# A two-step S5 recurrence and a reordered opening in a two-layer decoder kernel

## The reference, cut to what matters

```python
mag = exp(lr * dt); abar_r = mag * cos(li * dt); abar_i = mag * sin(li * dt)
bbar_r = fr * br - fi * bi; bbar_i = fr * bi + fi * br     # per group and state
bu_r = einsum('bsgc,gpc->bsgp', ug, bbar_r)                # bu_i alike
x[s] = abar * x[s-1] + bu[s]                               # complex, 256 steps, as an associative scan
y = einsum(xr, c_re) - einsum(xi, c_im) + d_skip * ug
y = gelu(y); y * sigmoid(y @ w_glu + b_glu)
```

## Time and profile before

| | |
|---|---|
| runs | 1571.39, 1573.44, 1573.77 us; median 1573.44 |
| profiled execution | span 1566.3 us from first to last instruction; no separate device time is kept for it, so 7.1 us of the median lie around its span |
| busy | PE 95%, DVE 82%, ACT 66%, POOL 7% |
| mean granted TensorE clock | 0.986 |
| chain that ended last | PE 80%, DVE 5%, ACT 4% |

### The profile page before, as it was taken

How to read it: one execution, slowest core, us unless ns; L and a number is a source line. 1 busy time by engine, 2 the same in 40 slices (tenths; PEclk the granted TensorE clock), 3 DMA queues, 4 the chain that set the end, 5 groups by cost and what they waited for, 6 DMA issues and landing times.

```text
span 1566.3 us, 21687 instructions
## 1 busy us (share of the span) xinstructions
PE 1489.2 (95%) x7201; PEld 1160.6 (74%) x7202; DVE 1288.4 (82%) x1776; ACT 1027.9 (66%) x1325; POOL 113.8 (7%) x112
## 2 busy tenths in 40 slices
PE   3999999999899899999999999999999999999987
PEld 1645468888795478878888888888888888888865
DVE  6896458785586369899999999989989989989987
ACT  3104444443456457887787788787888888888765
POOL 5251000000000000000001001001001001001030
PEclk9899999999899999999999999999999999999998
DMA  9733968874564289999999999999999999999960
GB/s 309 274 108 138 386 253 294 310 257 161 190 215 164 106 315 392 389 339 386 386 348 384 390 346 379 389 356 373 384 358 373 385 365 368 387 365 367 383 232 28
DMA packets 209930, 482.81 MB, mean 308 GB/s; under 512 B 8084, under 2 KB 14534, under 8 KB 209750
## 3 DMA queue, kind: packets, MB, share of 16 engines
q1 hardware_dynamic: 205872, 468.91, 81.3%
q0 software_dynamic: 3360, 12.10, 2.1%
q10 hardware_dynamic: 646, 1.16, 0.3%
HBM read 474.27 MB, written 7.86 MB: 308 GB/s over the span
## 4 chain that ended last, share of the span: by engine, by line
PE 80%; DVE 5%; ACT 4%; issue 2%; DVEq 0%; ACTq 0%
PE ps L864 23%; PE ps L866 23%; PE ps L865 23%; PE ps L870 3%; DVE w_lo L2056 3%; PE ps L1399 2%; PE ps L1156 2%; ACT work L1947 1%; PE ps L889 1%; ACT w_hi L1686 1%; PE ps L1127 0%; PE ps L958 0%; PE ps L1345 0%; ACT uT L1699 0%; PE ps L984 0%
## 5 line engine op out<-in xcount | busy, mean ns | idle before, releaser
L2056 DVE TENSOR_TENSOR w_lo<-ring,w_hi 128x1024 fp32r<-128x1024 f32 (+2 forms) x572 | 676.5, 1214 | 80.6 <-ACT w_hi L1686 61.7
L1686 ACT ACTIVATE w_hi<-ring 128x1024 fp32r<-128x1024 f32 (+2 forms) x572 | 596.0, 1052 | 222.6 <-PE ps L866 220.6
L864 PE MATMUL ps<-w_hi,e_hi 128*128 128x512 f32 x896 | 356.2, 398 | 5.5 <-DVE w_lo L2056 5.5
L866 PE MATMUL ps<-w_hi,e_lo 128*128 128x512 f32 x896 | 349.5, 390 | 0.0
L865 PE MATMUL ps<-w_lo,e_hi 128*128 128x512 f32 x896 | 348.8, 389 | 0.0
L2056 DVE TENSOR_TENSOR w_lo<-ring_more,w_hi 128x1024 fp32r<-128x1024 f32 x192 | 232.1, 1223 | 16.0 <-ACT w_hi L1686 7.0
L1686 ACT ACTIVATE w_hi<-ring_more 128x1024 fp32r<-128x1024 f32 x192 | 202.7, 1060 | 47.6 <-PE ps L866 47.6
L864 PEld LDWEIGHTS ps<-w_hi,e_hi 128*128 128x128 f32 x896 | 168.3, 188 | 42.1 <-DVE w_lo L2056 9.6
L866 PEld LDWEIGHTS ps<-w_hi,e_lo 128*128 128x128 f32 x896 | 168.1, 188 | 36.1
L865 PEld LDWEIGHTS ps<-w_lo,e_hi 128*128 128x128 f32 x896 | 168.5, 188 | 32.7
L864 PE MATMUL ps<-w_hi,eT_hi 128*128 128x512 f32 x448 | 176.7, 395 | 12.6 <-DVE w_lo L2056 12.6
(11 more groups left out here) (308 smaller groups left out, 1579.8 us busy)
## 6 DMA issues: line engine op xcount, KB each, us to landing
ring<-in_moe_w_gate SPq DMA_DIRECT2D x96, 1024.0 KB, 7.2
ring<-in_moe_w_up SPq DMA_DIRECT2D x80, 1024.0 KB, 7.2
ring<-in_moe_w_down SPq DMA_DIRECT2D x64, 1024.0 KB, 7.2
ring<-in_w_ada SPq DMA_DIRECT2D x24, 2048.0 KB, 12.6
ring_more<-in_moe_w_down SPq DMA_DIRECT2D x48, 1024.0 KB, 7.5
ring_more<-in_moe_w_up SPq DMA_DIRECT2D x32, 1024.0 KB, 7.6
ring_more<-in_moe_w_gate SPq DMA_DIRECT2D x16, 1024.0 KB, 7.6
ring<-in_ff_w_gate SPq DMA_DIRECT2D x5, 2048.0 KB, 8.2
```

Of the source, the lines that this page charges most:

```text
L864: mm(o, xh, wh, start=start, stop=False)
L866: return mm(o, xl, wh, start=False, stop=stop)
L1686: fn(w, src, ACT.Copy).then_inc(hi_ready, 1)
L2056: V.tensor_tensor(w_lo[0:n, c, 0:f], src, w_hi[0:n, c, 0:f].bitcast(F32), ALU.subtract).then_inc(lo_ready, 1)
```

## The change

In the S5 stage two steps of the recurrence are taken as one. With u split into even and odd steps, the state at odd steps obeys x[2k+1] = abar^2 x[2k-1] + (abar * bbar) u[2k] + bbar u[2k+1]; the scan has 128 steps (HS), the tables have 128 columns with doubled angle (so the levels are 0 to 6), and the factor is mag^2. The outputs at odd steps come from C x, those at even steps from (C * abar) x of the step before plus a direct product (C * bbar) u. So `drive(jp)` makes 8 products of 128 columns for the two chunks j0 and j0 + 4 of a pair, `turn(jp)` handles both, and `read_out(jp0)` has 36 products of 127 or 128 columns, four times instead of eight. New are: `ab_bar` and `ca` on POOL, `ab_pads` and `s5_direct_out` on ScalarE, `s5_direct` on TensorE, and two more weights (8 transposes) in `s5_transposes`.

The opening is reordered: SP starts with the conditioning items and loads x before the fourth; c, a_re, a_im, log_dt, b_ada and the small table go to ACT's queue; POOL loads the S5 matrices before the router's weights. TensorE gets 68 products of the identity by itself (`keep_busy`) between the conditioning products, `norm_first` comes after `matvec(3)`, and `s5_transposes` after `s_proj(1)`.

```diff
@@ sync
-            small("c", A["c"]); small("a_re", ...); small("a_im", ...)
-            sp.dma_start(bias_rows[0:BROWS, :], ...)
             for e in static_before[:n_first]:
+                if e is static_before[n_first - 2]:
+                    sp.dma_start(h[:, :, :], x_tok).then_inc(x_in, 16)
                 load(e)
@@ gpsimd (C and B are loaded ahead of w_r and b_r)
+            mul(par(MAG2), par(MAG), par(MAG))
...
+            for i, (x, y, op) in enumerate(((0, 1, ALU.subtract), (1, 0, ALU.add))):
+                mul(s5_t, f(AI), b_bar[:, y, :, :])
+                mul(ab_bar[:, i, :, :], f(AR), b_bar[:, x, :, :])
+                step.wait()
+                nc.gpsimd.tensor_tensor(ab_bar[:, i, :, :], ab_bar[:, i, :, :], s5_t, op).then_inc(ab_ready, 1)
+            pool.wait_ge(s5_wT_ready, 5)
...
+            mul(ca_t, fw(AI), mci)          # each of the next is 128 x 512
+            mul(ca[0], fw(AR), cr)
+            add(ca[0], ca[0], ca_t)
+            affine(ca[1], ca[0], -1.0, 0.0)
+            mul(ca_t, fw(AI), cr)
+            mul(ca[2], fw(AR), mci)
+            nc.gpsimd.tensor_tensor(ca[2], ca[2], ca_t, ALU.subtract).then_inc(ca_ready, 1)
+            for jp in range(NJP):           # 8 pairs, two 128 x 512 products each
...
@@ tensor
             def s5_transposes():
                 pe.wait_ge(s5_pads, 8)
-                for i, bank in enumerate((5, 6, 7, 4)):
+                for i, bank in enumerate((5, 6, 7, 4, 5, 6)):
...
+                    if i == 4:
+                        pe.wait_ge(s5_pads, 12)
+                        pe.wait_ge(s5_wT_ready, 2)
+            def keep_busy(n, bank):
+                for _ in range(n):
+                    mm(ps[bank][:, 0:P], ident, ident, start=True, stop=True)
             matvec(0, 4)
+            keep_busy(6, 2)
+            columns_of(0, parts0[:, 0, :], 4, 0)
+            keep_busy(10, 2)
             matvec(1, 5)
-            columns_of(0, parts0[:, 0, :], 4, 0)
-            norm_first()
+            keep_busy(6, 2)
+            columns_of(1, parts0[:, 1, :], 4, 4)
+            keep_busy(10, 2)
             pe.wait_ge(s5_dt, 1)
             matvec(2, 6)
-            columns_of(1, parts0[:, 1, :], 4, 4)
+            keep_busy(6, 2)
+            columns_of(2, parts0[:, 2, :], 4, 8)
+            keep_busy(30, 2)
             matvec(3, 7)
-            columns_of(2, parts0[:, 2, :], 4, 8)
+            norm_first()
             columns_of(3, parts0[:, 3, :], 4, 12).then_inc(mod_summed, 1)
-            pe.wait_ge(part_ready, 4)
-            s5_transposes()
...
+            def s5_direct():
+                pe.wait_ge(s5_wT_ready, 5)
+                for t in range(4):
+                    o = ps[7][:, t * P:(t + 1) * P]
+                    mm(o, b_pad[:, 0, t, :], s5_cT[:, 0, t, :], start=True, stop=False)
+                    w = mm(o, b_pad[:, 1, t, :], s5_cT[:, 2, t, :], start=False, stop=True)
+            def drive(jp):
...
+                for n, j in enumerate(j_pair(jp)):     # j0 = (jp // 4) * 8 + jp % 4, and j0 + 4
+                    t, r = j // 4, slice(32 * (j % 4), 32 * (j % 4) + 32)
+                    u = halves_of(t, r)                # s_inT[r, t, :] as even and odd steps
+                    for i in range(2):
+                        o = bank[:, (2 * n + i) * HS:(2 * n + i + 1) * HS]
+                        mm(o, s5_abT[r, i, t, :], u[:, 0, :], start=True, stop=False, tile_position=(r.start, 0))
+                        w = mm(o, s5_bT[r, i, t, :], u[:, 1, :], start=False, stop=True, tile_position=(r.start, 0))
+            def read_out(jp0):                         # waits: post_ready; ca_ready, k_ready (0); y_pre 2 (4)
+                for n in range(2):
+                    for jp in pairs: mm(o, s5_kT[:, t, r], halves_of(t, slice(0, P))[:, 0, :], ...)
+                    for i in range(4): for jp in pairs: mm(o, s5_caT[:, c, t, r], x[:, 0:HS - 1], ...)
+                    for i in range(4): for jp in pairs: mm(o, s5_cT[:, c, t, r], x, ...)
             s_proj(0)
             s_proj(1)
+            s5_transposes()
             s_proj(2)
+            s5_direct()
             drive(0)
-            drive(1)
             s_proj(3)
-            drive(2)
-            for jp in range(8):
-                for s in range(6 * jp, 6 * jp + 6):
+            drive(1)
+            for i in range(8):
+                for s in range(6 * i, 6 * i + 6):
                     qkv(s)
-                for j in (2 * jp + 3, 2 * jp + 4): ... drive(j)
-                if jp:
-                    read_out(2 * jp - 2)
+                if i + 2 < NJP:
+                    drive(i + 2)
+                if i in (2, 4, 6):
+                    read_out(i - 2)
             qk_transposes(0)
             qk_transposes(1)
             scores_pair(0, qT, kT, 0, True)
-            read_out(NCH - 2)
+            read_out(NJP - 2)
@@ scalar: order of the opening
-            norm_stats(0); part_out(0), (1); pads(); part_out(2), (3); norm_first_out(); s5_weights(); s_in copies
+            part_out(0), (1); c_pads(); roots(); part_out(2); norm_stats(0); b_pads(); part_out(3)
+            norm_first_out(); ab_pads(); s_in_out(0); s5_weights(range(7)); s5_direct_out(); s_in_out(1)
@@ vector
-            for n in range(5, NLEV): level(n)          # columns and norm_first_out inside level(7)
+            level(5); columns(0, 0, 1, 4); norm_first_out(); level(6)
-                    w = V.tensor_tensor_scan(z[:, i, :], ... MAG ... [P, S], ...)        # 2 of 256 a chunk
+                        w = V.tensor_tensor_scan(z[:, n, i, :], ... MAG2 ... [P, HS], ...)   # 4 of 128 a pair
+            y_before_gelu(0), (1) after turn(6); (2), (3) after the first two mask_max
```

More of the change, by code:

```diff
@@ L257, in trunk @@
         pT = WU.take(2, KW)
-        phase = phase_buf[:, :, :].rearrange("p a (b c) -> p a b c", b=NCH)
+        phase = phase_buf[:, 0, :].rearrange("p (a b c) -> p a b c", a=2, b=NCH)
+        WS = Region(phase_buf[:, 1, :], SLOT)
+        s5_abT = WS.take(2, 4, P)
+        s5_caT = WS.take(3, 4, P)
+        ab_pad = WS.take(2, 4, P)
+        ab_bar = WS.take(2, NCH, C_S5)
         WI = Region(ada[:, 2 * 4 * S:2 * 4 * S + 2048], 2048)
@@ L296, in trunk @@
         late_in = sem("late_in")
-        fill = [sem(f"slot{i}_filled") for i in range(NS1)]
+        fill = [sem(f"slot{i}_filled") for i in range(NS0)]
         half_fill = [[sem(f"slot{i}_half{j}_filled") for j in range(2)] for i in range(NS1)]
@@ L1047, in drive, with halves_of @@
+            def halves_of(t, r):
+                return s_inT[r, t, :].rearrange("p (k l) -> p l k", l=2)
+            def drive(jp):
+                if jp == 0:
+                    pe.wait_ge(s5_wT_ready, 7)
                     pe.wait_ge(vs_ready, 1)
[L1048 removed]
+                if jp == 4:
                     pe.wait_ge(vs_ready, 2)
[L1050 to L1055 removed]
@@ L1400, in o_out_part @@
                 w.then_inc(mix_out_done, 1)
-            def keep_busy(n, bank):
-                for _ in range(n):
-                    mm(ps[bank][:, 0:P], ident, ident, start=True, stop=True)
             def router(t):
@@ L2219, in _ @@
                 norm_scale(0, t, t + 1)
-            for n in range(5, NLEV):
-                level(n)
+            level(5)
+            columns(0, 0, 1, 4)
+            dve.wait_ge(mod_ready, 1)
+            norm_first_out()
+            level(6)
             def rope0(i):
@@ L2253, in turn @@
+                if jp >= 2:
+                    dve.wait_ge(post_ready, jp - 1)
+                z = zbuf[:, jp % 2]
+                for n, j in enumerate(j_pair(jp)):
+                    for i in range(2):
+                        w = V.tensor_tensor_scan(z[:, n, i, :], s5_p[:, MAG2, j:j + 1].broadcast_to([P, HS]), s5_v2[:, n, i, :],
+                                                 0.0, ALU.mult, ALU.add)
+                        if (n, i) != (1, 1):
+                            step(w)
                 w.then_inc(z_ready, 1)
-                dve.wait_ge(z_ready, j + 1)
+                dve.wait_ge(z_ready, jp + 1)
@@ L2259, in y_before_gelu @@
                                        ALU.mult, ALU.add).then_inc(y_pre, 1)
-            for j in range(NCH):
-                turn(j)
-                if j % 4 == 2 and j >= 6:
-                    y_before_gelu(j // 4 - 1)
-                if j in (7, 8, 12, 13):
-                    rope0({7: 0, 8: 1, 12: 2, 13: 3}[j])
+            for jp in range(NJP):
+                turn(jp)
+                if jp in (3, 4):
+                    rope0(jp - 3)
+                if jp == 6:
+                    y_before_gelu(0)
+                    y_before_gelu(1)
+                if jp in (6, 7):
+                    rope0(jp - 4)
```

228 lines of the change are left out of this document (127 added, 101 removed).

## The result

| | before | after |
|---|---|---|
| first comparison, median (runs) | 1573.49 us (1571.39 to 1573.77, 4) | 1585.74 us (1584.10 to 1587.30, 4) |
| ratio, 95% interval | | 1.0078 [1.0064, 1.0092] |
| repeated later | 1572.63 us (11 runs) | 1584.42 us (6 runs), 1.0073 [1.0055, 1.0091] |
| span of the profiled execution | 1566.3 us | 1585.5 us |
| mean granted TensorE clock | 0.986 | 0.984 |

A forecast was written before the change was run, and what follows sets the result against it. TensorE was taken to set the S5 stage, with VectorE costing it 1.8 us. Stage plus 9.8 and opening plus 1.6 gave plus 11.4 on 1573.4: 1584.8, say 1584.5 us; range 1573 to 1594.

The forecast's parts named there:

- VectorE costs the stage 1.8 us and its relief is worth no more: S5 stage: TensorE waits for VectorE only twice, 0.67 and 1.08 us; about 30 us less VectorE work saves only 1.8.
- Drives plus 4.8: S5 drives on TensorE: eight pairs at 1.93 us in one row group, 15.4 against 10.6 before, plus 4.8 us.
- Read-outs plus 1.6: S5 read-outs on TensorE: four at 4.1 us, 16.4, against eight at 1.85, 14.8; plus 1.6 us.
- Transposes plus 2.95, direct product plus 1.8: S5 stage on TensorE: 24 transposes now between two projections add 2.95 us, the direct product's 16 records 1.8.
- The tail plus 0.45: End of the S5 stage before the GLU: both last sums wait for the last read-out, plus 0.45 us.
- Stage plus 9.8: First S5 projection to GLU: all stage terms sum to plus 9.8 us; plus 6.8 by lower bounds, plus 22 by upper.
- The opening plus 1.6: Before the first S5 projection: identity products exceed the waits they fill, the clock wins back 2.8 us, start 1.6 us later.
- An opening that gains: Rival, opening: fillers fit into waits and DMA sets the fourth matvec, minus 4.6 us, total 1578.5; chance 0.2.
- Dear short products: Rival, S5 stage: weight loads exposed make short products cost more than the router's, total 1590 to 1597; chance 0.12.
- VectorE as the bound: Rival, S5 stage: VectorE sets the pace, so halved turns start the GLU 24 us earlier, total 1549; chance 0.15.
- Scans that do not get shorter: Rival, VectorE's turns: two scans of 128 cost one of 256, VectorE keeps 73 us, time as forecast; no chance given.
- The 7.1 us: Whole kernel: the profiled span of 1566.3 us was 7.1 under the runs' median, and the forecast added 11.4 to 1573.4.

The follow-up runs named there:

- experiment 2: Kernel before with VectorE's four rotary steps each replaced by a copy, so its output differs; 1565.73 us against 1573.43, ratio 0.9951.
- experiment 4: Kernel after with one multiplication in each VectorE turn done four times instead of once; 1585.18 us, ratio 1.0077 to the kernel before.
- experiment 5: Kernel after with the drives of two neighbouring pairs interleaved product by product, in two row groups; 1573.61 us, ratio 1.0000 to the kernel before.
- experiment 8: Kernel after with ten more identity products where TensorE waits for uT; 1579.26 us, ratio 1.0059 to the kernel before.
- experiment 6: Kernel after with two read-outs of four pairs, using four column groups, instead of four of two pairs; 1572.97 us, ratio 1.0012 to the kernel before.
- experiment 1: Kernel before, unchanged, executed once more for a second trace; 1567.82 us, span 1566.0 us.
- experiment 7: Kernel after without the 68 identity products of the opening; 1581.17 us, ratio 1.0069 to the kernel before.
- experiment 12: Kernel after, unchanged, run again for a second trace; 1584.42 us, stage from 48.81 to 150.06.

## Why the prediction was right

Point by point, with its own steps:
- **VectorE costs the stage 1.8 us and its relief is worth no more.** Right in kind. Its work fell by 31.8 us (about 30 forecast) and the stage grew; experiment 2 took work from it in the kernel before, experiment 4 gave it work in the kernel after, and TensorE's blocks did not move. The two waits cost 2.9 and not 1.8, because the first also parted a pair of drives (experiment 2). The sum does not suffer: that 1.0 is in its price of the old drives, four single ones at 1.05.
- **Drives plus 4.8.** Right: 2.01 a pair for the 1.93 of the sum, 8 x 2.01 = 16.1 against 10.6, plus 5.5. That the pairing by j0 + 4 is the reason is shown by experiment 5: the same products, alternating between two row groups, cost half. The rule of the Trainium skill that the prediction weighed (TensorEngine Tiling, Array Packing, section Tiling Modes: different tiles work in parallel) agrees with 2.01 us for one pair and for two.
- **Read-outs plus 1.6.** Right: 4 x 4.05 = 16.2, plus 1.4.
- **Transposes plus 2.95, direct product plus 1.8.** Right: 60.67 - 57.80 = 2.87, and 1.88. POOL's part was hidden.
- **The tail plus 0.45.** Right: from the end of the last read-out to the GLU 1.51 us (148.83 to 150.34) for 1.11 before (136.19 to 137.30), plus 0.40.
- **Stage plus 9.8.** Measured plus 11.2. (By the stated lower bounds the sum is 7.0, not 6.8; nothing rests on it.) The step that fails is the clock. The fillers did hold the 2.4 GHz level up to the fourth matvec, as the sum has it (1.92 a matvec at 23.97, 30.70 and 41.90), and the prediction had 1.00 from there on, and behind the wait for uT that it itself wrote down (2.26) the clock fell, 1.7 us. With that filled (experiment 8) the stage is 99.6, plus 9.6.
- **The opening plus 1.6.** Measured plus 1.8 (49.10) and, in the second trace, 1.5 (48.81); with the same opening and another stage it was 49.40, 49.54 and 51.34 (experiments 4, 5 and 6), so the 0.2 is luck. Two terms missed and cancelled: the start (14 forecast, 15.52) and the queue to the fourth matvec (27.2 forecast, 26.4), partly because the first six fillers took 1.45 and not 2.0; behind it 7.2 for 7.7. The reason for the start was wrong too: c was expected at 11, and the rows were turned at 14.48.
- **The rivals.** An opening that gains: no, the fillers exceeded the waits, as forecast. Dear short products: 0.111 a record held. VectorE as the bound: no. Scans that do not get shorter: 405 ns for 729, and it did not matter.

The 7.1 us that the prediction puts around the span are 1.8 (experiment 1); it added a difference to the median, so this did no harm. The forecast total came out as close as it did (1.2 us) partly by luck: the clock dip was missing from the sum, and behind the GLU the totals wander by more than that. The spans of the first two traces differ by 19.2, the GLU by 13.0 and the medians by 12.3. The chances for slower rested on the stage, and that held.

## What to carry to other kernels

Before work is moved between engines, read from the even period of the blocks whose queue it is: here VectorE at 92% was not the bound, and a relief of 32 us on it was worth at most 2.9, while the extra products and transposes on TensorE cost 12. If a rewrite makes products smaller, keep different row and column groups next to each other in the queue; either alone, the drives or the read-outs, turned plus 12 into nothing, and both with ten fillers into minus 8 (a part of these totals lies behind the stage; the stage went from plus 11.2 to minus 7.5). Filler products on TensorE belong only into waits that no other work fills: here 68 of them delayed the stage by 3.8 us, more than the half clock that they prevented, and ten in a wait kept the 1.7 us that a fall behind it costs.

## What was not expected of the hardware

- Four column groups, or two row groups, cost the time of half as many: 72 products of 128x32 in 4.08 us for 36 in 4.05, and 16 products with 32 rows in 2.01 for 8 in 2.01.
- A wait of 2.4 us on TensorE was followed by a clock of 0.50 in four traces of six. The low stretch lies behind the wait (50 to 53 in the kernel after); only with the wait of 5.4 us (experiment 7) did it begin inside, 0.50 from 43 on. Shorter waits were followed by it too, and not always: 1.31 us before the projection in experiment 2 but not in experiment 1, and 0.67 us in experiment 1 but not in the first trace of before.
- Small loads came late when the large ones were issued ahead of them on another queue: rows turned at 8.44 when three of them led SP's queue, and at 14.08 to 15.57 when all were on ACT's. From 2 to 8 us the DMA engines' share was 0.68 (139 GB/s) in the kernel before and 1.01 (320 GB/s) in the kernel after. With the three first on SP but without the rest of the old order it was 11.46 and 12.22. Several queues changed their order at once, so which of them it was is not shown.
- One program has clock falls at different places in different executions: the same wait, 1.7 us idle of 2, was followed by 0.50 once and by 1.00 once (experiment 12).
- Ahead of the first fall in a trace the granted clock of the rows is not to be relied on. In the kernel after it reads 1.00 from 15.5 to 19.0, where the first matvec takes 3.63 us for the 1.92 of the next ones; in experiment 7 it reads 1.00 from 16 to 34, and three matvecs there take 3.25 to 3.64. The time of a known group tells the level.
